# Differential-attention scores by query block, both maps of a head in one step, matmuls alternating between the two halves of the rows

## The chip, the cores and the metric

One core of one Trainium2 chip runs the whole kernel. The metric is the device time of one execution, in microseconds (us). Engines are named as in the profile: PE is TensorE's matmul side and PEld its weight loading, DVE is VectorE, ACT is ScalarE, POOL is GpSimd, SP issues the DMAs.

## The reference, cut to what matters

The kernel computes one decoder layer over 512 positions: three parallel branches (differential attention, gated DeltaNet, cross-attention to 256 memory tokens), their merge, an output projection and an MLP. The change touches only the scores of the differential attention:

```
s = einsum('bqhmd,bkhmd->bhmqk', qi, k) * 64 ** -0.5   # 8 heads h, two maps m, head size d = 64
s = s + bias[h]                                        # the same bias for both maps
s = where(dist >= 0, s, -inf)                          # causal
p = softmax(s)
w = p[:, :, 0] - lam * p[:, :, 1]                      # the two maps meet here
o = einsum('bhqk,bkhe->bqhe', w, v)
```

Each head has two score matrices (maps), 512 queries by 512 keys. Causality leaves, for the query block q (128 rows, q from 0 to 3), the first (q + 1) * 128 keys: 128, 256, 384 and 512 columns, 1280 for one map and 2560 for the head.

## The kernel before

**The stream of weight tiles.** Most of the work is a stream of 200 weight tiles (1024 x 128) that go through TensorE, each as 24 matmuls (lines 1541 to 1543: the weights and the activations are split into a high and a low part, which gives three products). A tile is loaded by SP, split by ACT (line 841, `w_hi`) and by DVE (line 1136, `w_lo`), and its result leaves the accumulator through ACT.

**Slots.** During the input projections the work is ordered by a plan made when the kernel is built (`plan_mixing`). In each slot TensorE does half a weight tile, then perhaps one step of DeltaNet (lists `DELTA`, PSUM tensor `ps_d`), then perhaps one step of attention (list `ATTN`, PSUM tensor `ps_a`, three banks of 512 columns). `COVER` says how many slots later the next step of the same list may be issued, 3 after `as0` and 4 after `as1`. Every engine walks through the same slots in order, and waits on semaphores: `a_mm` (a TensorE step of attention is done), `a_max` (the negated maxima are there), `a_act` and `a_dve` (ACT, DVE are done with a step). Before an attention step TensorE waits for `a_act` and `a_dve` of the steps before it, since they all use `ps_a`.

**One head of differential attention** is six steps: `av` (transpose of v), `as0`, `as1`, `at` (transposes of the weights, line 1622), `ap` (times v, line 1627), `ay` (transpose back, line 1631). Queries and keys of the head lie in `qkv_T` with the head size on the partitions: map 0 on rows 0 to 63, map 1 on rows 64 to 127. `as0` does the scores of map 0 and `as1` those of map 1, each with four matmuls (line 1616) of 64 contraction rows, in the order of query blocks 3, 2, 1, 0; they fill `ps_a` to 1280 of its 1536 columns. The stationary operand is the query block (64 x 128), the moving one the keys. Each f32 matmul stands in the trace as two records of LDWEIGHTS and two of MATMUL.

After the matmuls of such a step:

- DVE adds the bias strip to the last two key blocks of the three larger query blocks (line 1271, 768 columns) and to query block 0 (line 1272, 128 columns), takes four maxima (line 1274) and scales them into `nba` (line 1276). This is in the step's own slot.
- ACT does four exponentials with the row sums (line 964), one slot later (`EXP_LAG`).
- Two slots after `as1`, DVE forms p0/sum0 - lam * p1/sum1 (`attn_scale`, lines 1287 to 1297), for `at` to transpose.

DVE's and ACT's queues hold other work of the same slots: the DeltaNet step, the weight split, the causal convolution (lines 1230 and 1232) and its activation.

Of the kernel before, what the change touches and what calls it, by code (L numbers as in the profile page):

```python
# [29 lines left out]
P = 128  # L30
# [228 lines left out]
def build(nc, weights, x, mem, w_ba, params, consts, onehot, relb, post_g, y_dram, gate_dram, f_dram, frep_dram, out):  # L259
# [18 lines left out]
    with ExitStack() as ctx:  # L278
# [252 lines left out]
        BIAS_SLOTS = [9, 14, 20]  # L531
        GSUB, GDN = smd[:, 7:8], smd[:, 8:9]
        mxa, nba = smd[:, 16:20], smd[:, 20:24]
        sma, rca = smd[:, 24:32], smd[:, 32:40]
        ssa, rsa, tma = smd[:, 40:44], smd[:, 44:48], smd[:, 48:52]
        ssd, rsd, tmd = smd[:, 56:64], smd[:, 64:72], smd[:, 72:80]
# [3 lines left out]
        MEM_SLOTS = [3, 4]  # L540
        BA_SLOT, F_SLOT = 4, 6

        bank_of = {3: 0, 2: 512 + 128, 1: 1024 + 256, 0: 512}
        pack_of = {0: 0, 1: P, 2: 3 * P, 3: 6 * P}


# [287 lines left out]
        def _(act):  # L834
# [101 lines left out]
            def attn(i):  # L936
                kind, h = ATTN[i]
                act.wait_ge(a_mm, i + 1)
                if kind == "mv":
                    last = nc.scalar.copy(mv_tok[:, :, h * 512:(h + 1) * 512], ps_a[:, 0:2])  # L940
                elif kind == "cs":
                    act.wait_ge(a_max, n_max[i + 1])
                    for s in range(ST):
                        last = nc.scalar.activation(p_c[:, s], ps_a[:, s // 2, (s % 2) * MEM:(s % 2 + 1) * MEM],
                                                    ACT.Exp, bias=nba[:, s:s + 1], scale=SC_C,
                                                    accum_out=sma[:, s:s + 1])
                elif kind == "ct":
                    last = nc.scalar.copy(pT_c[:], ps_a[:, 0:2])
                elif kind in ("cv", "ay"):
                    if n_spill[i]:  # L950
                        act.wait_ge(y_out, 16 * n_spill[i])
                    if kind == "cv":
                        last = nc.scalar.copy(y_st[:], ps_a[:, 0:2])
                    else:
                        last = nc.scalar.activation(y_st[:, 0], ps_a[:, 0], ACT.Copy, scale=GSUB)
                elif kind == "av":
                    last = nc.scalar.copy(v_tok[:], ps_a[:, 0])
                elif kind in ("as0", "as1"):
                    m = int(kind[2])
                    act.wait_ge(a_max, n_max[i + 1])  # L960
                    for q in range(ST):
                        w = (q + 1) * P
                        src = flat(ps_a[:])[:, bank_of[q]:bank_of[q] + w]
                        last = nc.scalar.activation(p_a[:, m, pack_of[q]:pack_of[q] + w], src, ACT.Exp,
                                                    bias=nba[:, q:q + 1], scale=SC_A,
                                                    accum_out=sma[:, 4 * m + q:4 * m + q + 1])
                elif kind == "at":
                    nc.scalar.copy(wT[:, 0:1024], two(ps_a))
                    last = nc.scalar.copy(wT[:, 1024:1280], ps_a[:, 2, 256:512])
                elif kind == "ap":  # L970
                    last = nc.scalar.copy(flat(o_a[:]), ps_a[:, 0])
                last.then_inc(a_act, 1)
# [136 lines left out]
        def _(dve):  # L1109
# [145 lines left out]
            def attn(i):  # L1255

                kind, h = ATTN[i]
                if kind not in EXP_KINDS:
                    return
                dve.wait_ge(a_mm, i + 1)  # L1260
                if kind == "cs":
                    link(V_.reduce_max(mxa, two(ps_a).rearrange("p (a b) -> p a b", a=ST), AX_X))
                    V_.tensor_scalar(nba, mxa, -SC_C, None, ALU.mult).then_inc(a_max, 1)
                else:
                    if (kind, h) == ("as0", 0):
                        dve.wait_ge(strip_in, 16)
                        link(V_.tensor_tensor(strip[:, :, P:2 * P], strip[:, :, P:2 * P],
                                              over(cst[:, C_CAUS, :], HA), ALU.add))
                    ps = flat(ps_a[:])
                    near = view(ps, [[512, 3], [1, 2 * P]], 256)  # L1270
                    V_.tensor_tensor(near, near, over(strip[:, h], 3), ALU.add)
                    link(V_.tensor_tensor(ps[:, 512:512 + P], ps[:, 512:512 + P], strip[:, h, P:2 * P], ALU.add))
                    for q in range(ST):
                        ins = V_.reduce_max(mxa[:, q:q + 1], ps[:, bank_of[q]:bank_of[q] + (q + 1) * P], AX_X)
                    link(ins)
                    V_.tensor_scalar(nba, mxa, -SC_A, None, ALU.mult).then_inc(a_max, 1)

            def attn_scale(i):

# [209 lines left out]
        def _(pe):  # L1489
# [88 lines left out]
            def attn(i):  # L1578
                kind, h = ATTN[i]
                if i:  # L1580
                    pe.wait_ge(a_act, aA[i])
                    if aD[i]:
                        pe.wait_ge(a_dve, aD[i])
                if kind == "mv":
                    if h == 0:
                        pe.wait_ge(acc_free, TILES.index(("mv", KT - 1)) + 1)
                    for j in range(4):
                        for mt in range(MT):
                            last = nc.tensor.transpose(ps_a[:, mt, j * P:(j + 1) * P],
                                                       mv_T[:, 4 * h + j, mt * P:(mt + 1) * P], ident)  # L1590
                elif kind == "cs":
                    pe.wait_ge(acc_free, TILES.index(("cq", 2 * h + 1)) + 1)
                    for s in range(ST):
                        for dt in range(2):
                            last = mm(ps_a[:, s // 2, (s % 2) * MEM:(s % 2 + 1) * MEM],  # L1595
                                      cq_T[:, h % 2, dt, s * P:(s + 1) * P], mk_T[:, 2 * h + dt],
                                      start=dt == 0, stop=dt == 1)
                elif kind == "ct":
                    for mt in range(MT):
                        for s in range(ST):  # L1600
                            last = nc.tensor.transpose(ps_a[:, mt, s * P:(s + 1) * P],
                                                       p_c[:, s, mt * P:(mt + 1) * P], ident)
                elif kind == "cv":
                    for dt in range(2):
                        for mt in range(MT):
                            last = mm(ps_a[:, dt], mv_tok[:, mt, (2 * h + dt) * P:(2 * h + dt + 1) * P], pT_c[:, mt],  # L1606
                                      start=mt == 0, stop=mt == MT - 1)
                elif kind == "av":
                    pe.wait_ge(acc_free, TILES.index(("av", h)) + 1)
                    for s in range(ST):  # L1610
                        last = nc.tensor.transpose(ps_a[:, 0, s * P:(s + 1) * P], qkv_T[:, h % 2, 2, s * P:(s + 1) * P], ident)
                elif kind in ("as0", "as1"):
                    rows_m = slice(DA * int(kind[2]), DA * int(kind[2]) + DA)
                    ps = flat(ps_a[:])
                    for q in range(ST - 1, -1, -1):
                        last = mm(ps[:, bank_of[q]:bank_of[q] + (q + 1) * P], qkv_T[rows_m, h % 2, 0, q * P:(q + 1) * P],  # L1616
                                  qkv_T[rows_m, h % 2, 1, 0:(q + 1) * P], start=True, stop=True)
                elif kind == "at":
                    ps = flat(ps_a[:])
                    for kt in range(ST):  # L1620
                        for q in range(kt, ST):
                            last = nc.tensor.transpose(ps[:, t_bank(kt, q):t_bank(kt, q) + P],
                                                       p_a[:, 0, pack_of[q] + kt * P:pack_of[q] + (kt + 1) * P], ident)
                elif kind == "ap":
                    for q in range(ST):
                        for kt in range(q + 1):
                            last = mm(ps_a[:, 0, q * P:(q + 1) * P], wT[:, t_pack(kt, q):t_pack(kt, q) + P],  # L1627
                                      v_tok[:, kt * P:(kt + 1) * P], start=kt == 0, stop=kt == q)
                elif kind == "ay":
                    for q in range(ST):  # L1630
                        last = nc.tensor.transpose(ps_a[:, 0, q * P:(q + 1) * P], o_a[:, q], ident)
                last.then_inc(a_mm, 1)
# [303 lines left out]
```

## Time and profile before

| | us |
|---|---|
| median of three runs (lowest, highest) | 1498.67 (1494.84, 1499.0) |
| the profiled execution | 1497.8 |
| its span, first to last instruction | 1496.0 |
| PE busy | 1432.0 (96%) |
| DVE busy | 773.1 (52%) |
| ACT busy | 482.7 (32%) |
| granted TensorE clock, mean | 0.982 |

The span is what the views of the trace divide up; the profiled execution's own time is 1.8 us longer. Busy time is the time in which an engine has an instruction under way, and overlaps between instructions of one engine are counted once. The chain of waits is the sequence of work that ended last, followed back from the end of the execution: only time that stands in it can shorten the execution when it is taken away.

### The profile page before, as it was taken

Reading aid. Unit: us, or ns where it says so; the run is one execution under the profiler, and the core shown is the slowest. Engines: PE = TensorE matmul, PEld = TensorE weight load, DVE = VectorE, ACT = ScalarE, POOL = GpSimd, SP = SyncE. Lnnn points to the kernel's source line nnn. Section 1 sums busy time; section 2 is a strip of 40 time slices with the busy share of each in tenths; the row PEclk is TensorE's granted clock in tenths of the full one; section 3 lists DMA queues with packets and bytes.
Section 4 is the critical chain, followed back from the end, with each engine's and each line's share of the span. In section 5 each row is a group of like instructions: output and inputs, shape, how many; then the busy total and the mean of one; then the engine's idle time right before and its main releaser. Section 6 shows DMA issues by size and latency. Waiting matters only on the chain.

```text
span 1496.0 us, 18535 instructions
## 1 busy us (share of the span) xinstructions
PE 1432.0 (96%) x7540; PEld 1200.0 (80%) x7540; DVE 773.1 (52%) x1243; ACT 482.7 (32%) x762; POOL 258.7 (17%) x180
## 2 busy tenths in 40 slices
PE   5879999989999999999899999999979999999998
PEld 5679878768887778888688888888878888888887
DVE  6775236643367676754765334355355533255333
ACT  4334333333243343343343322111243221122221
POOL 2003210005200013100014231223232210022110
PEclk9989999999999999999999999999989999999998
DMA  5243121213111212102312255554412222323221
GB/s 197 69 163 122 64 85 57 85 43 120 57 52 55 78 38 83 62 31 71 106 50 71 92 164 175 189 184 148 168 54 82 97 87 87 111 85 99 97 86 57
DMA packets 46412, 142.77 MB, mean 95 GB/s; under 512 B 4944, under 2 KB 7416, under 8 KB 46328
## 3 DMA queue, kind: packets, MB, share of 16 engines
q1 hardware_dynamic: 46328, 141.59, 28.0%
q8 instruction: 60, 0.98, 0.3%
q14 instruction: 24, 0.20, 0.0%
HBM read 126.88 MB, written 16.27 MB: 96 GB/s over the span
## 4 chain that ended last, share of the span: by engine, by line
PE 82%; DVE 11%; ACT 3%; DMA 2%; issue 2%; SPq 0%; DVEq 0%; POOL 0%; ACTq 0%
PE acc L1541 21%; PE acc L1543 21%; PE acc L1542 21%; PE ps_d L1670 5%; PE ps_a L1616 2%; PE ps_d L1661 2%; DVE conv_y L1232 2%; PE ps_d L1675 2%; DVE w_lo L1136 2%; DMA w_raw<-weights 2%; ACT w_hi L841 1%; PE ps_a L1606 1%; PE ps_a L1627 1%; PE ps_a L1595 1%; PE ps_d L1664 1%
## 5 line engine op out<-in xcount | busy, mean ns | idle before, releaser
L1541 PE MATMUL acc<-n_hi,w_hi 128*128 128x512 f32 (+1 forms) x984 | 399.8, 406 | 6.7 <-DVE n_lo L1161 4.3
L1136 DVE TENSOR_TENSOR w_lo<-w_raw,w_hi 128x1024 fp32r<-128x1024 f32 x200 | 289.0, 1453 | 190.8 <-ACT w_hi L841 190.5
L1542 PE MATMUL acc<-n_lo,w_hi 128*128 128x512 f32 (+1 forms) x984 | 383.8, 390 | 0.0
L1543 PE MATMUL acc<-n_hi,w_lo 128*128 128x512 f32 (+1 forms) x984 | 383.8, 390 | 0.0
L841 ACT CAST w_hi<-w_raw 128x1024 fp32r<-128x1024 f32 x200 | 209.5, 1047 | 249.2 <-PE acc L1543 232.4
L1541 PEld LDWEIGHTS acc<-n_hi,w_hi 128*128 128x128 f32 x984 | 188.6, 192 | 45.4 <-issue 6.4
L1543 PEld LDWEIGHTS acc<-n_hi,w_lo 128*128 128x128 f32 x984 | 187.8, 191 | 41.1
L1542 PEld LDWEIGHTS acc<-n_lo,w_hi 128*128 128x128 f32 x984 | 188.7, 192 | 35.6 <-issue 1.0
L1543 PE MATMUL acc<-h_hi,w_lo 128*128 128x512 f32 x256 | 101.1, 395 | 0.0
L1541 PE MATMUL acc<-h_hi,w_hi 128*128 128x512 f32 x256 | 101.1, 395 | 0.0
L1542 PE MATMUL acc<-h_lo,w_hi 128*128 128x512 f32 x256 | 101.1, 395 | 0.0
L829 POOL TENSOR_TENSOR h_lo<-sq,h_hi 128x512 fp32r<-128x512 f32 x32 | 41.4, 1294 | 234.2 <-DVE h_hi L1472 234.2
L1541 PE MATMUL acc<-y_hi,w_hi 128*128 128x512 f32 x192 | 76.1, 396 | 0.0
L1543 PE MATMUL acc<-y_hi,w_lo 128*128 128x512 f32 x192 | 76.0, 396 | 0.0
L1542 PE MATMUL acc<-y_lo,w_hi 128*128 128x512 f32 x192 | 76.0, 396 | 0.0
L1081 ACT ACTIVATE sq<-relu 128x512 f32<-128x512 f32 x32 | 20.3, 634 | 126.1 <-DVE relu L1470 126.1
L1543 PEld LDWEIGHTS acc<-h_hi,w_lo 128*128 128x128 f32 x256 | 48.0, 188 | 11.7
L1541 PEld LDWEIGHTS acc<-h_hi,w_hi 128*128 128x128 f32 x256 | 48.0, 188 | 11.7
L1542 PEld LDWEIGHTS acc<-h_lo,w_hi 128*128 128x128 f32 x256 | 48.0, 188 | 11.7
L1232 DVE SCALAR_TENSOR_TENSOR conv_y<-conv_x,par,conv_y 128x512 f32<-128x512 f32 x72 | 54.1, 752 | 2.6
L1670 PEld LDWEIGHTS ps_d<-d_TT,d_KTT 128*128 128x128 f32 x384 | 46.5, 192 | 2.3 <-ACT d_KTT L987 0.3
L1541 PE MATMUL acc<-m_hi,w_hi 128*128 128x256 f32 x128 | 39.3, 307 | 9.1 <-DVE w_lo L1136 5.4
(311 smaller groups left out, 2056.5 us busy)
## 6 DMA issues: line engine op xcount, KB each, us to landing
w_raw<-weights SPq DMA_DIRECT2D x200, 512.0 KB, 3.5
gate_scratch<-gate_st SPq DMA_DIRECT2D x24, 256.0 KB, 2.2
g_in<-gate_scratch SPq DMA_DIRECT2D x24, 256.0 KB, 3.8
y_raw<-y_scratch SPq DMA_DIRECT2D x16, 256.0 KB, 3.6
x_tok<-x SPq DMA_DIRECT2D x4, 512.0 KB, 5.3
y_scratch<-y_st SPq DMA_DIRECT2D x4, 512.0 KB, 3.3
y_scratch<-d_ET SPq DMA_DIRECT2D x4, 512.0 KB, 3.2
y_scratch<-y_st SPq DMA_DIRECT2D x8, 256.0 KB, 2.6
```

The lines of the kernel that those rows point to most:

```text
L829: nc.gpsimd.tensor_tensor(h_lo[:, f % 16], sq[:, f % 2], h_hi[:, f % 16].bitcast(F32), ALU.subtract).then_inc(hl_ok, 1)
L841: nc.scalar.copy(w_hi[:, t % SPL], w_raw[:, t % RAW]).then_inc(hi_ready, 1)
L1081: nc.scalar.activation(sq[:, f % 2], relu[:, f % 2], ACT.Square).then_inc(sq_ok, 1)
L1136: V_.tensor_tensor(w_lo[:, t % SPL], w_raw[:, t % RAW], w_hi[:, t % SPL].bitcast(F32), ALU.subtract).then_inc(lo_ready, 1)
L1232: ins = V_.scalar_tensor_tensor(out=y, in0=conv_x[:, n % 2, j:j + S], scalar=par[:, col + j:col + j + 1], in1=y, op0=ALU.mult, op1=ALU.add)
L1541: mm(bank, wh, hi_of(k), start=start and k == 0, stop=False)
L1542: mm(bank, wh, lo_of(k), start=False, stop=False)
L1543: last = mm(bank, wl, hi_of(k), start=False, stop=stop and k == KT - 1)
L1616: last = mm(ps[:, bank_of[q]:bank_of[q] + (q + 1) * P], qkv_T[rows_m, h % 2, 0, q * P:(q + 1) * P], qkv_T[rows_m, h % 2, 1, 0:(q + 1) * P] ...
L1661: last = nc.tensor.transpose(dst[m], src[:, m], ident)
L1670: last = mm(ps_d[:, 0, m * P // 2:(m + 1) * P // 2], a[:, m], halves(b[:, m], c, second), start=True, stop=True)
L1675: last = mm(dst[m], a[:, m], b[:, m], start=True, stop=True)
```

## The change

The two attention score steps of a head keep their places in the plan, but their content is dealt out by query block instead of by map. `as0` now computes query block 3 of both maps and query block 1 of map 0 (512 + 512 + 256 = 1280 columns, three matmuls); `as1` computes query block 2 of both maps, block 1 of map 1 and block 0 of both (384 + 384 + 256 + 128 + 128 = 1280 columns, five matmuls). In the issued order each matmul takes its 64 contraction rows from the other half of the partitions than the one before it: map 0, 1, 0 and map 1, 0, 1, 0, 1. `score_parts` lists map, query block and first column in `ps_a`; neighbouring matmuls write different banks.

In `as0` DVE adds the bias once (768 columns) and takes three maxima; in `as1` it adds to 768 columns and then to both blocks 0 (256 columns), and takes five maxima. ACT does three exponentials, then five. The maxima and their negatives move to 16 other columns of `smd`. Everything after the exponentials is unchanged.

```diff
@@ in build @@
+        mxs, nbs = smd[:, 80:88], smd[:, 88:96]
-        bank_of = {3: 0, 2: 512 + 128, 1: 1024 + 256, 0: 512}
+        score_parts = {"as0": ((0, 3, 0), (1, 3, 512), (0, 1, 1280)),
+                       "as1": ((1, 2, 640), (0, 2, 128), (1, 1, 1280), (0, 0, 0), (1, 0, 512))}
+        score_cols = {"as0": slice(0, 3), "as1": slice(3, 8)}
@@ ACT, attn @@
-                    m = int(kind[2])
                     act.wait_ge(a_max, n_max[i + 1])
-                    for q in range(ST):
+                    for n, (m, q, col) in enumerate(score_parts[kind], score_cols[kind].start):
                         w = (q + 1) * P
-                        src = flat(ps_a[:])[:, bank_of[q]:bank_of[q] + w]
-                        last = nc.scalar.activation(p_a[:, m, pack_of[q]:pack_of[q] + w], src, ACT.Exp,
-                                                    bias=nba[:, q:q + 1], scale=SC_A,
+                        last = nc.scalar.activation(p_a[:, m, pack_of[q]:pack_of[q] + w],
+                                                    flat(ps_a[:])[:, col:col + w], ACT.Exp,
+                                                    bias=nbs[:, n:n + 1], scale=SC_A,
                                                     accum_out=sma[:, 4 * m + q:4 * m + q + 1])
@@ DVE, attn @@
                     near = view(ps, [[512, 3], [1, 2 * P]], 256)
-                    V_.tensor_tensor(near, near, over(strip[:, h], 3), ALU.add)
-                    link(V_.tensor_tensor(ps[:, 512:512 + P], ps[:, 512:512 + P], strip[:, h, P:2 * P], ALU.add))
-                    for q in range(ST):
-                        ins = V_.reduce_max(mxa[:, q:q + 1], ps[:, bank_of[q]:bank_of[q] + (q + 1) * P], AX_X)
+                    ins = V_.tensor_tensor(near, near, over(strip[:, h], 3), ALU.add)
+                    if kind == "as1":
+                        top = view(ps, [[512, 2], [1, P]])
+                        ins = V_.tensor_tensor(top, top, over(strip[:, h, P:2 * P], 2), ALU.add)
                     link(ins)
-                    V_.tensor_scalar(nba, mxa, -SC_A, None, ALU.mult).then_inc(a_max, 1)
+                    for n, (m, q, col) in enumerate(score_parts[kind], score_cols[kind].start):
+                        ins = V_.reduce_max(mxs[:, n:n + 1], ps[:, col:col + (q + 1) * P], AX_X)
+                    link(ins)
+                    V_.tensor_scalar(nbs[:, score_cols[kind]], mxs[:, score_cols[kind]], -SC_A, None,
+                                     ALU.mult).then_inc(a_max, 1)
@@ TensorE, attn @@
-                    rows_m = slice(DA * int(kind[2]), DA * int(kind[2]) + DA)
                     ps = flat(ps_a[:])
-                    for q in range(ST - 1, -1, -1):
-                        last = mm(ps[:, bank_of[q]:bank_of[q] + (q + 1) * P], qkv_T[rows_m, h % 2, 0, q * P:(q + 1) * P],
+                    for m, q, col in score_parts[kind]:
+                        rows_m = slice(DA * m, DA * m + DA)
+                        last = mm(ps[:, col:col + (q + 1) * P], qkv_T[rows_m, h % 2, 0, q * P:(q + 1) * P],
                                   qkv_T[rows_m, h % 2, 1, 0:(q + 1) * P], start=True, stop=True)
```

## Rows read from the trace of the kernel before

**Rows 1.** The page's busy times: us, share of the span, instructions.

```profile
PE 1432.0 (96%) x7540; PEld 1200.0 (80%) x7540; DVE 773.1 (52%) x1243; ACT 482.7 (32%) x762; POOL 258.7 (17%) x180
```

**Rows 2.** Busy us in 390 to 520: PE, PEld, DVE, ACT, POOL; PEclk, DMA, GB/s.

```profile
390.00:520.00 130.00, 126.36 (x700) 104.86 (x700) 84.95 (x176) 48.22 (x97) 8.17 (x6) 1.00 0.18 59
```

**Rows 3.** The score matmuls' line: duration ns min/median/max, first and last start.

```profile
L1616 PE MATMUL ps_a<-qkv_T x128: 269/448/693, 391.0 to 818.4; 64*128 64x512 f32 x32, 64*128 64x384 f32 x32, 64*128 64x256 f32 x32, 64*128 64x128 f32 x32
```

**Rows 4.** Chain of waits, first and last of 14 score steps: start, us.

```profile
391.04 2.35 PE ps_a L1616 x8
...
816.28 2.35 PE ps_a L1616 x8
```

**Rows 5.** PE, in order of time, merged, around a score step of head 4.

```profile
640.21 0.39 PE L1543 MATMUL acc<-n_hi,w_lo 128*128 128x512 f32 x1
...
642.60 2.42 PE L1616 MATMUL ps_a<-qkv_T 64*128 64x512 f32 x8
644.95 0.50 PE L1541 MATMUL acc<-n_hi,w_hi 128*128 128x512 f32 x1
```

**Rows 6.** PEld, the weight loads of the same step.

```profile
642.60 0.29 PEld L1616 LDWEIGHTS ps_a<-qkv_T 64*128 64x128 f32 x2
643.13 0.19 PEld L1616 LDWEIGHTS ps_a<-qkv_T 64*128 64x128 f32 x1 [0.24 <-issue]
643.56 1.26 PEld L1616 LDWEIGHTS ps_a<-qkv_T 64*128 64x128 f32 x5 [0.24 <-issue]
```

**Rows 7.** PE, a DeltaNet step ahead of the stream, and one ahead of scores.

```profile
656.06 1.89 PE L1670 MATMUL ps_d<-d_QT,d_SCR 128*128 128x64 f32 x16
657.76 0.48 PE L1541 MATMUL acc<-n_hi,w_hi 128*128 128x512 f32 x1
...
814.38 1.89 PE L1670 MATMUL ps_d<-d_QT,d_SCR 128*128 128x64 f32 x16
816.21 2.42 PE L1616 MATMUL ps_a<-qkv_T 64*128 64x512 f32 x8
```

**Rows 8.** Groups by shape, 390 to 830 us: busy us, mean ns of one.

```profile
L1274 DVE TENSOR_REDUCE smd<-ps_a 128x1 f32<-128x512 f32 x16 | 10.9, 681 | 0.0
L1274 DVE TENSOR_REDUCE smd<-ps_a 128x1 f32<-128x384 f32 x16 | 8.8, 548 | 0.0
L1274 DVE TENSOR_REDUCE smd<-ps_a 128x1 f32<-128x128 f32 x16 | 4.7, 292 | 0.5
L964 ACT ACTIVATE p_a<-ps_a,smd 128x512 f32<-128x512 f32 x16 | 11.2, 697 | 0.0
L964 ACT ACTIVATE p_a<-ps_a,smd 128x384 f32<-128x384 f32 x16 | 9.3, 584 | 0.0
L964 ACT ACTIVATE p_a<-ps_a,smd 128x128 f32<-128x128 f32 x16 | 5.9, 369 | 37.6 <-DVE smd L1276 37.6
```

**Rows 9.** Chain of waits: DVE and ACT on scores, heads 1, 2 and 4.

```profile
454.68 0.97 DVE ps_a L1271
...
470.58 0.87 DVE ps_a L1271
...
513.88 0.88 DVE ps_a L1271
...
629.04 0.97 DVE ps_a L1271
630.00 0.21 DVE ps_a L1272
...
630.24 1.70 DVE smd L1274 x4
...
636.83 1.88 ACT p_a L964 x7
...
640.67 2.00 PE ps_d L1670 x16
```

**Rows 10.** What ended PE's idle time, 390 to 830 us: us, times, longest.

```profile
PE ps_a L1622 <- DVE p_a L1295: 3.0, 1, 3.0
PE ps_a L1616 <- ACT p_a L964: 1.5, 1, 1.5
```

## The prediction

> **What bounds the kernel now.** I read the page's busy times first. The reader is to see TensorE busy for 96% of the span and the next engine, DVE, for 52% [rows 1]. Then the stretches in which the score steps lie: there DVE is busier than on average (85 of 130 us), but PE is still busy for 126 of 130 us, with the granted clock at 1.00, that is at its 2.4 GHz level [rows 2]. So the engine whose work the change reorders is the bound of its stretch.
>
> Next the lines of the score matmuls: 128 MATMUL records, two for each of 64 matmuls, 32 of each width, between 391 and 818 us [rows 3]. A busy share alone doesn't say that a shorter step shortens the run, so I followed the chain of waits: of the 16 score steps (two for each of 8 heads) 14 stand in it, each with its eight records and 2.35 us [rows 4]. They are 7 of the `as0` steps and 7 of the `as1` steps. The two that don't are the `as1` of head 1 at 467 us and the `as0` of head 2 at 506 us, where DVE and ACT work stands in the chain instead. All 16 together are 16 x 2.35 = 37.6 us, 2.5% of the span.
>
> Last, what one step consists of. It runs from 642.60 to 644.95 us, where the next work on PE starts [rows 5]. Within it the weight loads show the rhythm: two at the start, the third at 643.13, the fourth at 643.56 [rows 6]. A load goes ahead when the matmul before it starts, so 0.43 us is the time of one record of 512 columns: 0.83 ns a column, two cycles of 2.4 GHz. The 1280 columns of a step are in two records each, so 2 x 1280 x 0.833 ns = 2.13 us are pure streaming. The other 0.22 us are the first weight load, which nothing hides (the first interval is 0.53 instead of 0.43 us), and 0.11 us before the next work starts. So a score step is nearly nothing but streaming, with half of the array's rows idle in all of it: each matmul uses 64 of 128 rows.
>
> **The change, part by part.** TensorE: matmuls, records and columns remain: 8 matmuls and 2560 columns a head. In place of 4 + 4 there are 3 + 5. All that differs is which rows neighbours use. Before, each matmul of a step lay on the same 64 rows as the one before it, and could only follow it. Afterwards neighbours lie on different rows and write different banks. If the array lets them run beside each other, a step becomes shorter. The trace of before doesn't show it: in no place there does a matmul on rows 0 to 63 follow one on rows 64 to 127 directly. So the saving has to be bounded.
>
> Upper bound, each half of the rows takes its own records as soon as it is free: `as0` has on map 0's rows 512 + 256 columns and on map 1's 512, in two records each, and map 1 can't start before the second record of the first matmul. That gives 0.43 + 0.43 + 0.43 = 1.28 us in place of 2.13. `as1` has 384 + 256 + 128 columns on map 1's rows, 2 x 768 x 0.833 ns = 1.28 us, and the 512 of map 0 fit beside them. Each step saves 0.85 us.
>
> Closer bound, only the second record of one matmul and the first of the next lie beside each other: `as0` is 512, 512, 512 and 256 columns long, 1792 x 0.833 ns = 1.49 us, and saves 0.64. `as1` is 384 + 384 + 384 + 256 + 128 + 128 = 1664 columns, 1.39 us, and saves 0.75.
>
> Lower bound, nothing overlaps: saving 0. Below nothing: each change of rows costs something, priced under the rivals. Which value? What the trace shows is that a load overlaps a running matmul, and that the second half of the array has no work. With this I take overlap as likelier, and between its two bounds the middle. In the chain there are 7 + 7 steps: 7 x 0.64 + 7 x 0.75 = 9.7 us by the closer bound, 14 x 0.85 = 11.9 by the upper one, middle 10.8.
>
> Weight loads could become the limit when matmuls run beside each other. A DeltaNet step with 16 records of 64 columns, 0.05 us of streaming each, takes 1.70 us [rows 7]: 0.11 us a record, so that is the pace of loads. `as1` has ten of them, 1.1 us, less than 1.28, so I let them cost nothing. If they can't go ahead, each of the four short records at its end waits some 0.1 us, at most 0.4 us a step.
>
> Here a rule of the Trainium skill can be held against the rows. TensorE: Matmul & The Clock Gate, in Part 3 on packing, says that a weight load overlaps a matmul in flight only when the two lie on different row groups. The trace contradicts it for this kernel: the second load starts within the first matmul on the same rows [rows 6]. By the rule the before kernel would expose eight loads in each step and the change would hide most of them; the rows leave only the first one exposed, so nothing of that kind is to be won. The same part gives the start of a neighbour on other rows as about 4 ns later, and a speed-up of 3.07 for four tiles. No run here shows either yet.
>
> DVE: `as0` loses the add on 128 columns, which stands in the chain with 0.21 us beside the one before it [rows 9], and has maxima of 512, 512 and 256 columns instead of 512, 384, 256 and 128. Four maxima take 1.70 us in the chain while their durations add up to 1.94 us, so each gives back about 0.06 us by overlap: 0.62 - 0.49 - 0.23 = -0.10 us [rows 8, 9]. `as0` is 0.31 us shorter. `as1` is longer by 0.10 us for the maxima and some 0.13 us for 128 more columns in the second add (the maxima's 1.01 ns a column), 0.23 us together. ACT: an exponential with its read of the sum takes about its own duration, so `as0` loses 0.58 + 0.37 and gains 0.70 us, -0.26 us, and `as1` the opposite [rows 8].
>
> These count only where they are in the chain. DVE's and ACT's part of an `as0` step is there three times (heads 1, 2 and 4, at 455, 514 and 629 us), that of `as1` once, at 471 us, with DVE's part alone [rows 9]. In head 2 PE waits 1.5 us for these exponentials [rows 10], so the whole 0.57 us comes in; in head 1 as well. In head 4 PE itself arrives only 0.23 us before the step that waits (the stream's last matmul starts at 640.21 and streams 0.23 us, the waiting step starts at 640.67) [rows 5, 9], so only 0.23 comes in. Sum: -0.57 - 0.57 - 0.23 + 0.23 = -1.1 us.
>
> What is late next: the transposes of head 5 wait 3.0 us for DVE's scaling [rows 10], whose chain starts with a score step of PE and moves with it. Three places of such a kind are hidden in the stretch; I take off 1 us for paths which come up when PE gets earlier (ACT's and DVE's weight split, a weight load). No wait and no DMA is added or moved, and the slots don't change.
>
> Sum: -10.8 - 1.1 + 1 = -10.9 us. The profiled execution took 1497.8 us, 0.9 us below the median of the runs; 1498.7 - 10.9 = 1487.8, I say 1488 us (0.7% faster).
>
> **Rivals.** First, nothing overlaps: matmuls end in order and the array treats an f32 matmul of 64 rows as one over the whole array. For it speaks that f32 takes two records and two cycles a column, so that more than one product is in flight already; against it, that nothing in the rows needs the idle half. It leaves the 1.1 us of DVE and ACT: 1497.6 us.
>
> Second, on the other side: each change of rows drains the array. The trace has a price for going from 128 to 64 rows: a DeltaNet step of 16 records takes 1.70 us until the stream goes on, and 1.83 us until a score step starts; leaving the score step costs 0.11 us more [rows 5, 7]. Such a change costs 0.12 us, and 0.22 us if it also exposes the weight load. There are 2 changes in `as0` and 4 in `as1`, 42 in the chain: 42 x 0.22 = 9.2 us, less 1.1, is +8.1 us, 1507 us; at 0.12 us each it is +3.9 us, 1503 us. It decides from 0.13 us a change on. The Trainium skill speaks against it: TensorEngine Tiling (Array Packing), Key Properties, says that changing the tiling mode drains TensorE, not changing the tile. The entry into 64 rows above agrees with the first half of it; no row shows the second.
>
> Third, half of it: the overlap is there, but neighbours slow each other (both read moving data and write results at once), and half of 10.8 us is left: 1498.7 - 5.4 - 1.1 + 0.5 = 1492.7 us.
>
> **How the numbers follow.** Full overlap within the two bounds 0.52, half of it 0.10, none 0.24, drain 0.14. This kernel's measurement tells about 0.3%, 4.5 us, from no change. The full and the half case lie beyond it: faster 0.62. No overlap is the same: 0.24. Drain is slower: 0.14. The likeliest case alone has 1484 to 1491 (13.0 us at the upper bound and 2 us of scatter; 9.7 - 2 at the closer one). The range reaches to the case without overlap, with its scatter: 1483 to 1500.
>
> **What would show it.** A step of L1616 from its first record to the next work on PE: 1.5 us (own queue for each half) or 1.6 to 1.7 us (records in pairs) in place of 2.35; 2.35 means no overlap, 2.6 to 3.2 a drain. In the record starts, a map-1 record that starts beside a map-0 record. PE's busy time falls by 10 to 13 us. Maxima and exponentials of `as0` take 1.6 and 1.9 us, those of `as1` 1.8 and 2.4. The wait of the `as1` step at 519 us falls from 1.5 to about 0.9 us. Wrong would be the prediction if steps shorten and the time doesn't: then look for PE's idle time behind DVE between 455 and 485, 507 and 519 and 707 and 719 us.

## The result, and the profile after

| | before | after |
|---|---|---|
| median of the runs, us | 1498.37 (4 runs) | 1485.55 (4 runs) |
| profiled execution, us | 1497.8 | 1485.6 |
| its span | 1496.0 | 1483.8 |
| PE busy | 1432.0 | 1411.9 |
| DVE busy | 773.1 | 772.5 |
| 16 score steps together, first record to next work | 37.7 | 23.8 |

The ratio after to before is 0.9925, 95% interval 0.9903 to 0.9947: 0.75% faster, where 0.7% was forecast (1488 us). In two later sets of six runs the same kernel had medians of 1485.06 and 1485.11 us, with 0.9917 (0.9899 to 0.9935) and 0.9920 (0.9897 to 0.9943).

The page after, busy times as in [rows 1]. 8 instructions fewer on DVE, one a head:

```profile
PE 1411.9 (95%) x7540; PEld 1187.2 (80%) x7540; DVE 772.5 (52%) x1235; ACT 483.0 (33%) x762; POOL 259.3 (17%) x180
```

The steps of head 4 in the kernel after, PE in order of time (start, us, records), beside [rows 5]:

```profile
622.33 1.55 PE L1622 MATMUL ps_a<-qkv_T 64*128 64x512 f32 x6
623.82 0.50 PE L1547 MATMUL acc<-n_hi,w_hi 128*128 128x512 f32 x1
...
636.98 1.56 PE L1622 MATMUL ps_a<-qkv_T 64*128 64x384 f32 x10
638.47 0.50 PE L1547 MATMUL acc<-n_hi,w_hi 128*128 128x512 f32 x1
```

Both steps take 1.49 us to the next work in place of 2.35. The first 0.3 to 0.4 us alone show why. Kernel before, PE and PEld between 642.5 and 642.9 us: one matmul record runs, and two weight loads have been made.

```profile
642.60 0.69 PE L1616 MATMUL ps_a<-qkv_T 64*128 64x512 f32 x1
642.60 0.29 PEld L1616 LDWEIGHTS ps_a<-qkv_T 64*128 64x128 f32 x2
```

Kernel after, between 636.9 and 637.3 us: two records within one record's time, and four loads.

```profile
636.98 0.59 PE L1622 MATMUL ps_a<-qkv_T 64*128 64x384 f32 x2
636.98 0.30 PEld L1622 LDWEIGHTS ps_a<-qkv_T 64*128 64x128 f32 x4
```

The records' starts in the two steps, us from the first one:

```
first step   0.000 0.006 (block 3, both maps)  0.533 0.540  0.962 1.178 (block 1)
second step  0.000 0.007 (block 2, both maps)  0.427 0.433  0.749 0.756 0.865 0.965 1.181 1.290
```

Each half of the rows has a sequence of its own. In the second step map 1's records (0.000, 0.427, 0.749, 0.965, 1.181, 1.290) follow each other without a gap (the first load, which nothing hides, is in the first 0.427), map 0's (0.007, 0.433, 0.756, 0.865) run beside them, and the step is as long as the longer half.

Where the time came from can be read by place. The table has the start of a step on PE in the two traces, and their difference, at the end of each head's score work:

```
                       before    after   difference
first step,  head 0    390.97   391.63    +0.66
transposes,  head 0    426.03   424.97    -1.06
second step, head 1    467.40   465.20    -2.20
transposes,  head 1    485.35   483.12    -2.23
second step, head 2    519.34   516.64    -2.70
transposes,  head 2    542.54   540.03    -2.51
second step, head 3    580.50   577.08    -3.42
transposes,  head 3    600.25   595.98    -4.27
second step, head 4    642.60   636.98    -5.62
transposes,  head 4    662.37   655.91    -6.46
transposes,  head 5    718.92   710.73    -8.19
first step,  head 6    744.81   736.52    -8.29
second step, head 6    758.41   750.20    -8.21
transposes,  head 6    775.48   766.42    -9.06
transposes,  head 7    835.97   825.18   -10.79
end of the span       1496.01  1483.77   -12.24
```

From the first score step to the last transposes the difference grows by 11.45 us. The 0.66 us at the start have nothing to do with the change (nothing of it has run). The last 1.45 lie where the two programs are the same, and can't be put down to it either: in the variants below this tail is between 0.0 and 2.3 us shorter than in that one trace of before, 1.4 us in the one without any overlap.

These places are read from one trace of each kernel. In the two other traces of the changed kernel the stretch from the first score step to the last transposes is 13.41 and 13.75 us shorter than in before, not 11.45. The difference comes back below, under the account of the 14 steps.

### The profile page after: what moved, and what is told of

Same layout as the page of the kernel before. It is cut to its first block, busy times and chain, and to the rows that moved or that the text cites. A ratio compares the mean times of both kernels' runs of the same rounds, so it can differ in the third digit from the quotient of the medians.

```text
span 1483.8 us, 18527 instructions
## 1 busy us (share of the span) xinstructions
PE 1411.9 (95%) x7540; PEld 1187.2 (80%) x7540; DVE 772.5 (52%) x1235; ACT 483.0 (33%) x762; POOL 259.3 (17%) x180
## 4 chain that ended last, share of the span: by engine, by line
PE 82%; DVE 11%; ACT 3%; issue 2%; DMA 2%; SPq 0%; DVEq 0%; ACTq 0%
PE acc L1547 21%; PE acc L1549 21%; PE acc L1548 21%; PE ps_d L1676 5%; PE ps_d L1667 2%; DVE conv_y L1234 2%; PE ps_d L1681 2%; DVE w_lo L1138 2%; PE ps_a L1622 1%; DMA w_raw<-weights 1%; PE ps_a L1612 1%; ACT w_hi L844 1%; PE ps_a L1633 1%; PE ps_a L1601 1%; PE ps_d L1670 1%
## 5 line engine op out<-in xcount | busy, mean ns | idle before, releaser
L745 POOL TENSOR_TENSOR d_ET<-cst,gdec 128x1024 f32<-128x1024 f32 x4 | 8.5, 2118 | 223.3 <-PE ps_d L1662 223.3
```

## The experiments

All were compared with the kernel before on the same chip. "Step" is the time from a step's first record to the next work on PE.

**One half of the rows for all.** Map 1's blocks are computed from map 0's rows.

```diff
-                        rows_m = slice(DA * m, DA * m + DA)
+                        rows_m = slice(0, DA)
```

> The changed kernel, but every score matmul takes its 64 contraction rows from partitions 0 to 63, so map 1 gets map 0's scores; the grouping of maxima, adds and exponentials is that of the changed kernel. Theory (the two halves of the array work beside each other, and this is nearly all of the gain): no neighbours on different rows, so a score step is again 2.35 us (2.13 us of streaming, 0.11 for the first weight load, 0.11 at the end) in place of 1.49; 14 steps in the chain x 0.86 = 12.0 us more than the changed kernel, about 1497.5 us. Rival (the lighter first step on DVE and ACT, which other work waits for, brings it): the step is longer but the time stays within 1486 to 1490 us.

Median 1498.67 us, ratio 1.0003 (0.9983 to 1.0023). Steps 2.34 and 2.36 us:

```profile
625.94 2.41 PE L1622 MATMUL ps_a<-qkv_T 64*128 64x512 f32 x6
628.28 0.50 PE L1547 MATMUL acc<-n_hi,w_hi 128*128 128x512 f32 x1
628.62 0.39 PE L1548 MATMUL acc<-n_lo,w_hi 128*128 128x512 f32 x1
```

With only the grouping of the change, and no neighbours on different rows, nothing of the gain is left that the time could show. The trace does show the lighter first step: against before, the second steps of heads 1, 2 and 4 start 0.27, 0.34 and 0.51 us earlier, 1.1 us together.

**The kernel before, rows in turn.** Its own grouping, DVE and ACT untouched; blocks 2 and 0 get the other map's scores.

```diff
-                    rows_m = slice(DA * int(kind[2]), DA * int(kind[2]) + DA)
                     for q in range(ST - 1, -1, -1):
+                        m = (ST - 1 - q) % 2
+                        rows_m = slice(DA * m, DA * m + DA)
```

> The kernel before, with its own grouping (four query blocks of one map a step, DVE and ACT as before), but the four matmuls of a step take their 64 contraction rows in turn from partitions 0 to 63 and 64 to 127, so blocks 2 and 0 get the other map's scores. Columns on the two halves are 512 + 256 and 384 + 128 in each step. Theory: 2 x 768 columns x 0.833 ns = 1.28 us of streaming on the longer half, step 1.49 us, time that of the changed kernel plus what DVE and ACT bring there (0.4 to 1.1 us): 1486 to 1487 us. Rival (the regrouping on DVE and ACT brings it): 1497 to 1498 us.

Median 1487.21 us, ratio 0.9923 (0.9905 to 0.9940), steps 1.48 us (PE, head 4):

```profile
619.03 1.55 PE L1617 MATMUL ps_a<-qkv_T 64*128 64x512 f32 x8
620.51 0.50 PE L1541 MATMUL acc<-n_hi,w_hi 128*128 128x512 f32 x1
```

Two lines in TensorE's part have the gain. The two experiments together leave no room for the rival that DVE and ACT bring it: the time comes from the overlap. The grouping is what allows it with correct scores, since a step needs work of both maps for it.

The trace also tells how the end of such a step is signalled. The increment that DVE waits for hangs on the matmul issued last, block 0, whose second record starts 0.865 us into the step. Block 1 was issued before it on the other half, and its second record starts only at 1.178 us and takes 0.38 us. DVE, which had been waiting for 4.45 us, starts 1.61 us into the step, behind both:

```profile
620.64 0.97 DVE L1271 TENSOR_TENSOR ps_a<-ps_a,strip 128x768 f32<-128x768 f32 x1 [4.45 <-PE ps_a L1617]
```

So records of the two halves start independently, but the increment of the last matmul did not come ahead of an earlier one's end.

**The order within a step.**

```diff
-                    for m, q, col in score_parts[kind]:
+                    for m, q, col in BY_HALF[kind]:
+        BY_HALF = {"as0": ((1, 3, 512), (0, 3, 0), (0, 1, 1280)),
+                   "as1": ((0, 2, 128), (0, 0, 0), (1, 2, 640), (1, 1, 1280), (1, 0, 512))}
```

> The changed kernel with the same matmuls in each step, issued by half of the rows: first step map 1 block 3, then map 0 blocks 3 and 1; second step map 0 blocks 2 and 0, then map 1 blocks 2, 1 and 0. Theory A (each half takes its own records out of a window, whatever stands ahead of them for the other half): steps stay at 1.49 us, 1485.5 us. Theory B (matmuls start in issue order, only neighbours overlap): first step 0.43 + 1.28 + 0.22 = 1.93 us, second step 0.75 + 1.28 + 0.22 = 2.25 us, 7 x (0.44 + 0.76) = 8.4 us more, 1494 us.

Median 1486.24 us, ratio 0.9920 (0.9899 to 0.9940), steps 1.49 and 1.50 us. In the second step (PE and PEld, first 0.3 us) two records run at once, although two whole matmuls of map 0 stand ahead of map 1's first:

```profile
636.24 0.60 PE L1624 MATMUL ps_a<-qkv_T 64*128 64x384 f32 x2
...
636.24 0.31 PEld L1624 LDWEIGHTS ps_a<-qkv_T 64*128 64x128 f32 x4
```

The starts are 0.000, 0.013, 0.426, 0.440 us: map 1's first record starts at 0.013, and the second record of map 0's first matmul, issued before it, at 0.426. The widths confirm it. The records that start in the first 0.7 us are these, all of 384 columns, although two of 128 were issued before map 1's two of 384:

```profile
L1624 PE MATMUL ps_a<-qkv_T x4: 482/535/587, 636.2 to 636.7; 64*128 64x384 f32 x4
```

Theory A holds: matmuls for different halves need not be neighbours in the issued order. "Alternating" in the change is not what brings the time (1486.24 us here, where theory B had 1494); having both halves in one step is. The Trainium skill (TensorE: Matmul & The Clock Gate, Part 3, What overlaps and what doesn't) says that matmuls start and end strictly in program order. For f32 matmuls on two halves of the rows this trace disagrees about the starts, and the measurement decides. On completion no run disagrees: in the experiment before this one the increment of the last matmul waited for the earlier one.

**The halves balanced.** In the change one half has 768 columns in each step, the other 512. With 512 + 512 and 768 + 768 the two steps are shorter together. Block 1 of both maps then shares a bank, and the variant makes map 1's wait for map 0's; without the wait it was not tried. The adds, maxima and exponentials follow the new dealing: fewer in the first step, more in the second, and one add more.

```diff
+        score_parts = {"as0": ((0, 3, 0), (1, 3, 512)),
+                       "as1": ((0, 1, 1024), (1, 2, 640), (0, 2, 128), (1, 1, 1280), (0, 0, 0), (1, 0, 512))}
+                        if (m, q) == (1, 1):
+                            pe.wait_ge(a_one, h + 1)
...
+                        if (m, q) == (0, 1):
+                            last.then_inc(a_one, 1)
```

> The changed kernel with the halves of the rows balanced: first step block 3 of both maps (512 columns on each half), second step blocks 2, 1 and 0 of both maps (768 on each half), block 1 of both maps in one bank, so that TensorE itself waits on a semaphore for map 0's block 1 before it issues map 1's. One more add on DVE in the second step. Theory: first step 0.85 + 0.22 = 1.07 us, second 1.28 + 0.22 = 1.50, with 0.1 to 0.2 us for the wait and an unhidden weight load 1.65; 0.27 us less a head in 7 heads, less 0.3 us for DVE in the chain: 1484 us. Rival: the wait keeps all behind it from being issued until its semaphore is there, the second step is 1.9 us or more, and the time is 1485.5 to 1488 us.

Median 1482.39 us, ratio 0.9895 (0.9880 to 0.9911), steps 1.06 and 1.60 us. Head 4's second step on PE:

```profile
633.14 1.67 PE L1627 MATMUL ps_a<-qkv_T 64*128 64x256 f32 x12
634.74 0.50 PE L1550 MATMUL acc<-n_hi,w_hi 128*128 128x512 f32 x1
```

The wait itself costs nothing (map 1's block 1 starts at 0.757 us, when its half is free). The record behind it starts 0.10 us late (1.075 us instead of 0.757 + 0.215): its weight load could not go ahead of the wait, and begins at 0.861 us.

**All 128 rows.** Each block is the sum of both maps' products.

```diff
-                        rows_m = slice(DA * m, DA * m + DA)
+                        rows_m = slice(0, 2 * DA)
```

> The changed kernel, but every score matmul takes all 128 contraction rows, so each block is the sum of both maps' products. No step then uses 64-row tiles. Theory (going into and out of 64 rows costs time in itself): the first record follows the work before it without the 0.11 us, and the step ends without the other 0.11 us; 2.13 us of streaming plus at most the 0.11 us of the first weight load, 2.13 to 2.24 us to the next work. Rival (the two 0.11 us belong to any attention step, from its semaphores): 2.35 us, as with 64 rows on one half.

One run: 1488.04 us. The steps are 1.96 to 2.19 us to the next record, below the pure streaming: the next record's start stands early in the trace, and the measure I had chosen is no good. The start of the record after it is better (PE, the same step as in the first experiment):

```profile
622.45 2.37 PE L1622 MATMUL ps_a<-qkv_T 128*128 128x512 f32 x6
624.47 0.59 PE L1547 MATMUL acc<-n_hi,w_hi 128*128 128x512 f32 x1
624.89 0.39 PE L1548 MATMUL acc<-n_lo,w_hi 128*128 128x512 f32 x1
```

It is 2.44 us here and 2.68 us with 64 rows of one half (625.94 to 628.62), and the record before the step starts 0.11 instead of 0.20 us ahead of it. So going into 64 rows and out again costs 0.33 us a step, 0.39 us in the steps whose first weight load was hidden here. That is 5 to 6 us of both kernels, and the change leaves it. It is most of what makes this kernel, which has no overlap, as fast as it is: from the first score step to the last transposes its trace is 6.5 us shorter than before's, that of the first experiment 1.5. The Trainium skill (TensorEngine Tiling (Array Packing), Key Properties) says that a change of mode drains TensorE and a change of tile does not; the 0.33 us and the 0.007 us between two starts on different halves agree with the two.

**Four steps without the overlap.**

```diff
+                        half = 0 if (kind, h) in (("as1", 1), ("as0", 2), ("as0", 3), ("as1", 3)) else m
-                        rows_m = slice(DA * m, DA * m + DA)
+                        rows_m = slice(DA * half, DA * half + DA)
```

> The changed kernel with four score steps without overlap (all contraction rows from partitions 0 to 63, so map 1 of these blocks is map 0's): second step of head 1 and first step of head 2, which the chain of waits did not hold, and both steps of head 3, which it held. Theory (only steps in the chain count): all four are 2.35 us; compared step by step with the changed kernel, what follows the first two starts no later (within 0.1 us), what follows the other two starts 0.86 us later each, 1.7 us in all. Rival (TensorE is the bound everywhere, the chain is only one of many of equal length): 0.86 us later after each of the four, 3.4 us.

One run, 1482.92 us, which by its scatter says nothing on 1.7 us. The traces do. Part of the low time is the clock: between the first score step and the last transposes PE had 6.8 us at half clock (granted clock 0.50, the level of 1.2 GHz) in this trace and 10.2 us in that of the changed kernel. All four steps are 2.34 to 2.36 us. Against before, the start of what follows moved by -0.01 us over the second step of head 1 (after: -0.03), by -0.45 over the first of head 2 (after: -0.45), by -0.01 over the first of head 3 (after: -0.87) and by +0.02 over its second (after: -0.85). The theory holds to 0.03 us: the overlap was worth nothing in the two steps outside the chain of waits and all of its 0.86 us in the two of head 3. PE, head 3, both steps and the transposes, in this kernel and then in the kernel after:

```profile
560.62 2.41 PE L1623 MATMUL ps_a<-qkv_T 64*128 64x512 f32 x6
574.13 2.43 PE L1623 MATMUL ps_a<-qkv_T 64*128 64x384 f32 x10
593.90 1.26 PE L1629 MATMUL ps_a<-cst,p_a 128*128 128x128 f32 x10
```

```profile
564.43 1.55 PE L1622 MATMUL ps_a<-qkv_T 64*128 64x512 f32 x6
577.08 1.56 PE L1622 MATMUL ps_a<-qkv_T 64*128 64x384 f32 x10
595.98 1.26 PE L1628 MATMUL ps_a<-cst,p_a 128*128 128x128 f32 x10
```

From the first step to the transposes it is 33.28 us there and 31.55 us here.

**The changed kernel again**, unchanged.

> The changed kernel once more, beside the variants of this call. 1485.5 us, ratio to before 0.9915 to 0.993. If the gaps of TensorE that the profile puts down to nothing (2.57 us at 527 us, 2.73 at 533, 0.71 at 748) belong to this program, they come again at the same places; if they are chance, others come.

Median 1485.06 us (6 runs). The gaps come at the same places, so they belong to the program; what they are stands in the next section. Only the first has the same length: 2.57 us at 527, but 1.15 instead of 2.73 us at 534 and 1.41 instead of 0.71 us at 747.

```profile
527.40 1.60 PE L1662 MATMUL ps_d<-cst,conv_o 128*128 128x128 f32 x8 [2.57 <-issue]
...
533.99 2.02 PE L1670 MATMUL ps_d<-cst,d_ET 128*128 128x128 f32 x16 [1.15 <-issue]
```

Between the two gaps PE ran at half clock for 3.4 us here and at full clock in the first trace. It took 1.6 us more for the same work (527.40 to 532.85, against 526.55 to 530.41), and the gap behind it is 1.6 us shorter.

**The late wait.** The balanced kernel with its second step in another order.

```diff
-  "as1": ((0, 1, 1024), (1, 2, 640), (0, 2, 128), (1, 1, 1280), (0, 0, 0), (1, 0, 512))
+  "as1": ((0, 1, 1024), (1, 2, 640), (0, 2, 128), (1, 0, 512), (0, 0, 0), (1, 1, 1280))
```

> The balanced kernel with the wait of TensorE put behind all other matmuls of the second step: only map 1's block 1 is issued after it. Theory (the balanced step lost 0.11 us to a weight load that could not go ahead of the wait): second step 1.49 us in place of 1.60, 7 to 8 x 0.11 us less, about 1481.5 us, and 4 us below the changed kernel. Rival: the last load is exposed in the same way, 1.60 us, 1482.4 us.

Steps 1.06 and 1.50 us (head 4: 634.36 to 635.86), as expected. Median 1482.34 us (1479.44 to 1489.09, 6 runs), ratio 0.9909 (0.9885 to 0.9933): 2.7 us below the changed kernel beside it, where 4 were expected. By the time alone it can't be told from the rival's 1482.4; the length of the step decides.

**Both once more**, side by side.

> The changed kernel a third time, next to the balanced one below: 1485.3 us, the middle of the two medians so far, within 1 us.

> The balanced kernel with the late wait a second time. Its two score steps together are 2.56 us against 2.97 us in the changed kernel. Theory (about 12 of the 16 steps reach the end, six heads' worth): 6 x 0.41 = 2.5 us less, plus 0.3 us for the lighter first step on DVE and ACT: 1482.5 us, 2.8 us below the changed kernel of this call. Rival (the heavier second step on DVE gives it back, the 3 us so far are chance): within 1 us of it.

1485.11 us (6 runs, 0.9920, 0.9897 to 0.9943) and 1484.84 us (6 runs, 1479.47 to 1486.73; 0.9914, 0.9888 to 0.9939). The medians are 0.3 us apart, as the rival had it, the means 1.8 us with a standard error of 1.6. Over all runs the changed kernel has a mean of 1485.4 us (16 runs) and the balanced one, with either wait, 1483.2 us (16 runs); 2.2 us, with a standard error of 0.9 us. But four runs of each were not made side by side. The twelve and twelve that were differ by 1.6 us, with a standard error of 1.1. That the balanced version is the faster is likely and not shown. In the trace its two steps are 2.56 us where the change has 2.97.

## Why the prediction was right, step by step

- **The array lets the halves overlap.** Right, and at the upper bound: a step saves 0.86 us where the bounds were 0.64 to 0.85 and the middle 0.77 was taken. The closer bound rested on records starting in issue order; the order experiment shows that they don't.
- **14 of 16 steps count.** This was the mis-sized term: in this pair of traces 12 did. The two outside the chain gave nothing, as read. But the second step of head 2 and the first of head 6 gave nothing either, though both stood in the chain of before (and stand in that of after: a wait put down to "issue" does not lead the chain over to the engine that caused it). The place is the same in both: a DeltaNet step on PE waits for DVE. In the kernel after, DVE's two rows and the PE row that they release, at 525 us; then PE's at 748 us and the DVE row that ends just before it:

```profile
525.23 1.23 DVE L1334 TENSOR_TENSOR d_KB<-d_K,beta 128x1024 f32<-128x1024 f32 x1
...
526.55 1.06 PE L1662 MATMUL ps_d<-cst,conv_o 128*128 128x128 f32 x8 [2.57 <-issue]
...
746.94 1.22 DVE L1336 TENSOR_TENSOR d_V<-ps_d,hbeta 128x1024 f32<-128x1024 f32 x1
...
748.25 2.02 PE L1670 MATMUL ps_d<-cst,d_ET 128*128 128x128 f32 x16 [0.71 <-issue]
```

  The profile puts these gaps down to "issue". DVE ends at 526.46 and 748.16, PE starts 0.09 us later each time, and the wait is one that the code has (`d_dve`): it is DVE. When the changed kernel ran again, 0.85 us later at this place, it was the same (DVE ends at 527.31, PE starts at 527.40). In before, PE idled only 0.16 us at the first place, and so the chain ran through PE:

```profile
527.92 1.22 DVE L1328 TENSOR_TENSOR d_KB<-d_K,beta 128x1024 f32<-128x1024 f32 x1
...
529.25 1.06 PE L1656 MATMUL ps_d<-cst,conv_o 128*128 128x128 f32 x8 [0.16 <-issue]
```

  The slack of the next path was 0.16 us, and the step gave 0.86. I took 1 us off for paths that come up, without naming a place; 1.7 us were lost, at these two. At the second place this depends on the execution: in the traces of the order experiment and of the four steps there is no such gap, and the first step of head 6, which has the overlap in both, gave its 0.8 to 0.9 us.
- **A lower clock was part of that slack.** In before, PE ran at half clock behind its 1.5 us wait at 519 us; in after it didn't. Windows of the kernel before, then after (PEclk is the third number from the right):

```profile
521.90:524.50 2.60, 2.60 (x7) 2.08 (x7) 2.50 (x4) 0.00 (x0) 0.00 (x0) 0.50 0.00 0
```

```profile
518.20:524.00 5.80, 5.78 (x25) 4.38 (x24) 4.49 (x15) 2.26 (x3) 0.00 (x0) 1.00 0.05 20
```

  The full 2.4 GHz in the place of 1.2 saved PE 1.4 us there (of the difference, -3.70 at 521.8 us became -5.10 at 528.2), and all of it went into the 2.57 us wait for DVE: an earlier PE is worth nothing where DVE ends last.
- **The clock makes the rest of the difference between traces.** Behind the second wait for DVE in head 2, PE ran at half clock in before and in after, and at full clock when the changed kernel ran again. The windows of the three:

```profile
535.20:538.40 3.20, 2.76 (x13) 2.79 (x14) 3.08 (x10) 1.74 (x4) 0.00 (x0) 0.50 0.49 169
...
532.70:536.00 3.30, 2.86 (x13) 2.89 (x14) 2.94 (x10) 1.98 (x6) 0.00 (x0) 0.50 0.52 164
...
535.20:538.40 3.20, 3.20 (x19) 2.73 (x18) 3.16 (x7) 1.88 (x3) 0.00 (x0) 1.00 0.14 54
```

  The same work took 1.4 us less there, and 0.7 to 0.9 us more were gained around head 6, where before and after had half clock and the two other traces of the changed kernel had not. That is the way from 11.45 to 13.41 and 13.75 us. The count of 12 steps, and the sum below, hold for the pair of traces whose stretches at half clock lie at the same places but for the one at 521 us. What decides where they fall in an execution, and whether the change makes them fewer, is open.
- **DVE and ACT, -1.1 us.** Right in its sum, not in its parts: second steps of heads 1, 2 and 4 came 0.28, 0.45 and 0.51 us earlier beside the overlap (1.24 us, and 1.1 us in the experiment without overlap), where 0.57, 0.57 and 0.23 were forecast (1.37). The 0.23 us that the heavier second step was to cost in head 1 came as 0.19 us in head 2 instead, whose second wait for DVE has these rows before it. That leaves 1.05 us. The chain after, head 1's first and second step on DVE and ACT (beside [rows 9]; the second add of the second step was priced at 0.13 us more than 0.21 and took 0.34):

```profile
452.75 0.98 DVE ps_a L1273
453.75 1.63 DVE smd L1279 x3
...
460.39 1.81 ACT p_a L965 x6
...
468.15 0.87 DVE ps_a L1273
469.02 0.34 DVE ps_a L1276
469.39 1.76 DVE smd L1279 x5
```

- **The sum.** 12 x 0.86 + 1.24 - 0.19 = 11.4 us against 11.45 measured between the first score step and the last transposes of this pair. Forecast were 14 x 0.77 + 1.1 - 1 = 10.9. Two errors, a saving too small and two steps too many, nearly cancelled; that the number came out so well is luck. The medians differ by 12.8, 11.8 and 12.7 us in the three sets of runs. What they have beyond 11.4 can't be divided by steps: it is of the size of what the clock and the parts outside the stretch give or take between executions.
- **Signs that were named.** The steps' 1.49 us and the pairs of records came as forecast. PE's busy time fell by 20.1 us, not 10 to 13: 13.9 us are the score steps, 4.0 lie behind the last transposes, where the programs are the same. The wait of head 2's second step fell from 1.50 to 1.28 us, not to 0.9.
- **The rivals.** No overlap: excluded by records of both maps that start 0.007 us apart, and by the first two experiments. Drain at each change of rows: the start of a neighbour on other rows comes 0.007 us later, not 0.12 to 0.22. The price was real, but that of going from 128 to 64 rows and back, 0.33 to 0.39 us together. Neighbours slowing each other: map 1's records keep 0.32 us for 384 columns with map 0's beside them (0.427 to 0.749), the 0.83 ns a column of before.

## What to carry to other kernels

Matmuls with 64 contraction rows should have, in every stretch that TensorE works through at once, partners on the other half of the rows (here always in other banks), with equal columns on both halves; the order within the stretch made no difference of more than 0.02 us in a stretch of five. Before pricing such a saving by the chain of waits, look for the path next to it at each place: a step in the chain is worth only the slack of the second path, and a gap called "issue" may be a wait for an engine that ended just before. Before closing a sum to a tenth of a us on one pair of traces, look where each of them ran at half clock: three traces of one program differed by 2.3 us.

## What the runs showed of the hardware that was not expected

- An f32 matmul of 64 rows is issued as two records, and these go to their half of the array independently: two halves worked at full speed each (2.13 us of streaming became 1.28), out of issue order by at least two matmuls. The increment on the matmul issued last still came after the earlier one's end.
- Going from 128-row matmuls into 64-row ones and out again costs 0.33 to 0.39 us, about as much as one record of 512 columns takes (0.43 us).
- A wait on TensorE's own semaphore between its matmuls cost nothing by itself, but it kept back the next weight load, 0.11 us of the step (1.60 instead of 1.49 us); with the waiting matmul issued last the step took 1.50 us.
